# Loading each weight piece of the second tile as two transfers, of 120 and of 8 partitions

## The reference

```python
proj = h @ w_in[l]                       # 1024 x 2496, split into q_a, lat, ..., v_b, f_b
o_a = dsa_attention(...)                 # sparse attention, 8 heads
o_b = forgetting_attention(...)          # 8 heads
x = x + gate1 * (mixed @ w_out[l])       # 1024 x 1024
h2 = rms_norm(x, g_ffn[l]) * (1.0 + scale2) + shift2
x = x + gate2 * peer_ffn(h2, w_peer_q[l], keys1, keys2, peer_u[l], peer_v[l])
```

## Time and profile before

| what | value |
|---|---|
| runs, median (lowest to highest) | 1419.11 us (1418.01 to 1419.70) |
| the profiled execution's own time | 1418.62 us |
| its span, first to last instruction | 1416.6 us |
| what lies around the span | 2.0 us |
| PE busy | 1297.8 us, 92% |
| DVE busy | 833.9 us, 59% |
| POOL busy | 428.2 us, 30% |
| HBM read | 429.23 MB, 304 GB/s over the span |
| moved by POOL's queue (q0), by SP's queue (q1) | 275.99 MB, 154.50 MB |

### The profile page before, as it was taken

The page is one execution under the profiler, slowest core; times in us unless marked ns, Lnnn a source line. Parts: engine busy times, 40 slices in busy tenths (PEclk is TensorE's granted clock), DMA queues, the critical chain, the costliest instruction groups (busy, mean ns, idle before and its releaser), DMA issues.

```text
span 1416.6 us, 15143 instructions
## 1 busy us (share of the span) xinstructions
PE 1297.8 (92%) x5447; PEld 837.6 (59%) x5447; DVE 833.9 (59%) x2027; ACT 275.0 (19%) x670; POOL 428.2 (30%) x554
## 2 busy tenths in 40 slices
PE   7999999999999999999989999989997777777776
PEld 6888888888687777757666644445642222222222
DVE  3553466213138888733486678757666767766654
ACT  2013100130010000033333234432220112111101
POOL 0101030000100000000024455555566555655551
PEclk9999999999999999999999999999999999999999
DMA  8345665224468888577369999999999999999995
GB/s 290 121 159 190 230 139 179 79 101 149 134 238 316 291 314 290 185 263 280 120 273 423 422 424 420 422 411 410 425 425 425 425 426 424 426 425 426 425 427 229
DMA packets 120202, 431.46 MB, mean 305 GB/s; under 512 B 10950, under 2 KB 34956, under 8 KB 84544
## 3 DMA queue, kind: packets, MB, share of 16 engines
q0 software_dynamic: 37904, 275.99, 47.5%
q1 hardware_dynamic: 82224, 154.50, 30.2%
HBM read 429.23 MB, written 1.24 MB: 304 GB/s over the span
## 4 chain that ended last, share of the span: by engine, by line
PE 59%; DMA 29%; DVE 3%; issue 3%; POOL 3%; ACT 2%; SPq 0%; POOLq 0%; DVEq 0%; ACTq 0%
PE psum L588 31%; DMA wr<-peer_uv,arena 13%; DMA arena<-peer_uv,arena 9%; PE psum L1116 6%; PE psum L890 4%; DMA first_slot<-peer_uv,arena 4%; DMA xc<-peer_uv,arena 3%; PE psum L968 2%; PE psum L866 2%; PE psum L941 2%; PE psum L1134 1%; POOL arena L2566 1%; PE psum L639 1%; POOL wr L2594 1%; PE psum L1178 1%
## 5 line engine op out<-in xcount | busy, mean ns | idle before, releaser
L588 PE MATMUL psum<-hT,wr 128*128 128x256 f32 x1792 | 391.6, 380 | 1.8 <-DMA wr<-in_w_in 1.8
L588 PEld LDWEIGHTS psum<-hT,wr 128*128 128x128 f32 x1792 | 339.1, 190 | 51.7 <-issue 6.0
L1116 PE MATMUL psum<-wr,arena 128*128 128x512 f32 x576 | 276.0, 609 | 39.1 <-POOL arena L2566 38.9
L2392 DVE CUSTOM_DVE_ANT_0 wr<-psum,wr 128x1024 f32<-128x1024 f32 x144 | 176.1, 1223 | 108.8 <-DMA wr<-peer_uv,arena 108.6
L1116 PEld LDWEIGHTS psum<-wr,arena 128*128 128x128 f32 x576 | 102.6, 193 | 178.9 <-issue 177.7
L2566 POOL TENSOR_SCALAR arena<-cst,arena 128x128 f32<-128x128 f32 x256 | 121.4, 474 | 171.5 <-ACT arena L1544 163.3
L2594 POOL DMA_INDIRECT wr<-peer_uv,arena x144 | 144.0, 1000 | 84.5 <-PE psum L1116 60.7
L1116 PE MATMUL psum<-arena 128*128 128x512 f32 x256 | 125.9, 616 | 33.6 <-POOL arena L2566 33.6
L1544 ACT ACTIVATE arena<-arena 128x1 f32<-128x1 f32 x256 | 50.9, 202 | 488.1 <-DVE arena L2392 487.8
L2392 DVE CUSTOM_DVE_ANT_0 arena<-psum,arena 128x1024 f32<-128x1024 f32 x64 | 78.4, 1224 | 55.5 <-DMA arena<-peer_uv,arena 55.5
L1116 PEld LDWEIGHTS psum<-arena 128*128 128x128 f32 x256 | 44.2, 191 | 111.4 <-issue 111.3
(11 more groups left out here) (350 smaller groups left out, 1422.6 us busy)
## 6 DMA issues: line engine op xcount, KB each, us to landing
wr<-in_w_in SPq DMA_DIRECT2D x22, 2048.0 KB, 8.8
arena<-in_w_ada SPq DMA_DIRECT2D x12, 2048.0 KB, 9.9
wr<-in_w_up SPq DMA_DIRECT2D x22, 1024.0 KB, 8.3
arena<-piece SPq DMA_DIRECT2D x16, 1024.0 KB, 9.1
wr<-in_w_down SPq DMA_DIRECT2D x5, 2048.0 KB, 9.7
wr<-in_w_a_out SPq DMA_DIRECT2D x2, 2048.0 KB, 8.1
wr<-in_w_b_out SPq DMA_DIRECT2D x2, 2048.0 KB, 8.6
wr<-in_w_o SPq DMA_DIRECT2D x2, 2048.0 KB, 8.1
```

Source lines behind the costliest of these rows:

```text
L588: mm = nc.tensor.matmul(bank[p % 4][:, f * S:(f + 1) * S], slot(i)[:, k, n * P:(n + 1) * P], act[:, k, :], start=k == 0, stop=k == KT - 1)
L1116: mm = nc.tensor.matmul(bank[(6, 0)[t] + half][:, :], diag[:, n % DIAGS, :], gring[slot_of][:, D + half * BANK:D + (half + 1) * BANK], sta ...
L2392: V.tensor_tensor_reduce(gring[slot_of][:, 0:D], h2[t], gring[slot_of][:, 0:D], 1.0, 0.0, ALU.mult, ALU.add, dots[:, t, c:c + 1]).then_inc ...
```

## The change

SP gets a helper, `load_piece`, that issues two DMAs for a piece in place of one: partitions 0 to 119, then partitions 120 to 127. Both add 16 to the same semaphore, so PE waits for 32 a filling where it waited for 16. All 18 pieces are loaded in this way. Nothing else is changed: SP's waits, the places, and the programs of DVE, ACT and POOL stay, and PE's program differs in the number it waits for.

```diff
         @block.sync
         def _(sp):
+            def load_piece(j):
+
+                for r in (slice(0, 120), slice(120, P)):
+                    sp.dma_start(piece_land(j)[r], pieces[j][r]).then_inc(p_in[PIECE_PLACE[j][0]], 16)
+
...
                     for j in range(2):
-                        sp.dma_start(piece_land(j), pieces[j]).then_inc(p_in[j], 16)
+                        load_piece(j)
...
             for j in range(2, len(pieces)):
-                b, _, before = PIECE_PLACE[j]
+                _, _, before = PIECE_PLACE[j]
                 signal, count = ("pv_ready", UNITS) if before is None else PIECE_DONE[before]
                 sp.wait_ge(s[signal], count)
-                sp.dma_start(piece_land(j), pieces[j]).then_inc(p_in[b], 16)
+                load_piece(j)
...
             def landed_piece(j):
                 b, turn, _ = PIECE_PLACE[j]
-                pe.wait_ge(p_in[b], 16 * (turn + 1))
+                pe.wait_ge(p_in[b], 32 * (turn + 1))
                 return piece_at(j)
```

## The result

The changed kernel takes 1484.24 us, median of four runs (1482.24 to 1490.40), against 1419.40 for the kernel before, measured beside it (1418.01 to 1419.86): a ratio of 1.0462, 95% interval 1.0444 to 1.0481, so 65 us slower. The forecast was 1415.3 with a range of 1412.7 to 1421.4, so both its sign and its size are wrong. The profiled execution has a span of 1483.3 us.

What follows compares the result with a forecast made beforehand. The DMA engines were taken as the bound, one late engine ending the kernel. Terms of -4.4, +1.1 and -0.5 made -3.8 us, from a profiled 1418.62 to 1414.8, so runs at 1415.3, range 1412.7 to 1421.4.

Steps and rivals of the forecast that it cites:

- The change part by part: Pricing step: counted each engine's rows of a piece at 0.309 us each and summed the change to -3.8 us.
- Added to eight engines: Ninth row on eight engines for 13 pieces loaded beside gathers: 4.0 us at most, taken as +1.1 at the end.
- before gathers flow and have time: Pieces 0 to 4, loaded before the gathers flow: having time, they were priced at 0.
- eight-engine split: Pieces' 120 partitions go over only eight engines, 32 us late: 1451 us, chance 0.02, left out of the range.
- A's span: Run times if the relieved engine is the late one: 1413.7 to 1417.2 us, about 1415.3; chance 0.65.
- Case A's premise: At the gathers' end, the late engine is the one given no piece rows; its 4.4 us lag goes.
- lone stretch: End of gathers, about 1400.3 to 1404.9 us: one engine works alone at 26.5 GB/s; priced at 4.4 us.
- steps of 3.4 us: DVE's gather steps, five between 1060 and 1400 us instead of 2.48 us; read as the late engine fetching instructions.
- case C: Late engine keeps 8 rows, or 120 partitions use 16 engines: nothing changes, 1418.6 to 1419.7 us; chance 0.15.
- B: Late engine gets a ninth row, lengthening the gathers' end by 1.9 to 4.0 us: 1421.0 to 1423.1; chance 0.18.
- two signs of being wrong: The lone stretch goes without the time falling, or PE's wait for pieces grows beyond 2 us.
- theory C: For the shift by four: what counts is how many engines of a piece share a memory part; 1408 to 1412 us.

Runs made afterwards that it cites:

- split by columns: Kernel before with each piece loaded as two transfers of all 128 partitions, one for each half of the columns: 1419.95 us, ratio 1.0011.
- 60-partition run: Kernel before with only partitions 32 to 91 of each piece loaded, 4 rows on each of 15 engines: 1411.26 us, ratio 0.9924.
- shift by four: Kernel before with only partitions 36 to 99 of each piece loaded, the other half left out: 1420.93 us, ratio 1.0017.
- 32 to 95: Kernel before with only partitions 32 to 95 of each piece loaded, the other half left out: 1407.52 us, ratio 0.9921.

## Why the prediction was wrong

**The step that failed** is in "The change part by part": every row of a piece was priced at 0.309 us, wherever it lands and whatever lands beside it, and only the rows on each engine were counted. From that came "Added to eight engines: 0.309 us a piece, 13 x 0.309 = 4.0 us at most." The dealing itself fits: the page's packets rose from 120202 to 120328, by 126 = 18 x 7, which is 15 and 8 completions a piece in place of 16. But the price is off: from 777 to 795 us a packet of a gather took 0.470 us in place of 0.278. Three terms stood at nothing or next to it: the 120 partitions, 8 rows an engine "as before", cost 45 us; the 8 partitions, bounded by 4.0, cost 19 or 20; and within these sums the pieces that are loaded "before gathers flow and have time", put at 0, stand behind 4.8 of the 6.8 us by which the first gather is late in the profiled execution.

**The bounds** did not hold it either. For 120 partitions I bounded how many engines share the rows (16, 15, 8) and found the eight-engine split at 1451. I did not bound how long a row takes, though none of the rows I used shows a load of fewer than 128 partitions beside gathers; the earlier trace rows is one alone, and of 16 KB. The packet time was carried from whole loads to a form that the trace doesn't show. Two smaller slips bear on nothing: A's span lies 0.73 and not four fifths below 1416.27, so 0.48 and not 0.52 for faster; and from 920 to 960 us the rate fell by 4%, but the share by 2% only, so the engines ran dry for about half of what was credited.

**The rule against the change** (the Trainium skill, "DMA: Bandwidth & Descriptors", section "Rules for kernel authors") I put aside because its reason would hold only "where both parts divide by 16", at 0 to +4 us. The split into 64 and 64, which divides by 16 twice, costs 56 us. The advice, one transfer of 128, was right; the reason given there (the same engines serve both) is not why, as the split by columns shows, where the same is true and nothing is lost.

**Case A's premise**, that the relieved engine is the late one, has the runs against it too: the lone stretch is there in the 60-partition run and in the changed kernel at 1467 us, and the steps of 3.4 us, which A had "gone or rarer", are all five in the changed kernel, at the same gathers, from 1131.2 to 1407.0 us. A spared engine that keeps its lead would show none of it. With packets at full pace the change would then have been case C or B; no run shows that.

**What held**: the DMA engines are the bound from 745 us on, bytes are unchanged, and SP's extra issues cost nothing that the runs can tell (split by columns). One of the two signs of being wrong came true, PE's wait for pieces beyond 2 us; the lone stretch of about the old length was the sign of case C.

**What stays open.** Shown is that the cost hangs on which partitions a load names, with packets, bytes and engines held equal. That the engines meet at ports of on-chip memory is inferred from the Trainium skill's map; no row shows a port, or which engine takes which rows. The number of ports alone (theory C of the shift by four) failed there, and the second term, an engine's own place, was put forward with that run and has no other test. How much of the loss is each of the two terms isn't settled for 120 partitions.

## What to carry to other kernels

Where DMA engines are the bound, a load that names all 128 partitions is a different thing from the same rows in two loads: split by columns (free here) and not by partitions (26 to 65 us here). A DMA line at full share with a GB/s line that falls, at packets of the same size, says that packets have become slower; divide the share by the packets, for the queue that was not changed as well. And where an edit gives a transfer a shape that the trace doesn't show, bound the time of a packet, not only the number of them.

## What was not expected

Slow rows of one queue slow the other queue on the same engines: a gather's packets took 1.69 times as long beside pieces of 120 and 8 partitions. And not every load of less than 128 partitions is slow: 32 to 95 landed in 3.7 us at best and moved 414 GB/s from 750 to 1090 us, where the kernel before moved 421. The Trainium skill, "SBUF — State Buffer", section "Door 1: The DMA port swizzle (why [64,N] ≈ [32,N])", maps 32 to 95 onto all 16 ports, and the runs fit that. They don't fit the same page's sentence, in the section "Can I just issue two DMAs to hit both halves?", that only a transfer over all 128 partitions reaches them all.
